# First attention in two parts, three query tiles between the rounds of the last key choice, and the bias table made early

## The reference

```python
def dsa_mixer(h, rel_bias, w_in, ..., w_uq, w_q_idx, w_uk, w_uv, w_o):
    c_q, c_kv, k_idx, w_idx = split(h @ w_in)            # then each normed
    q = einsum('btr,rhd->bthd', c_q, w_uq)
    q_abs = einsum('bthd,chd->bthc', q, w_uk) * HEAD_DIM ** -0.5
    q_idx = einsum('btr,rhd->bthd', c_q, w_q_idx)
    def block(args):                                     # 128 queries
        rel = relu(einsum('bqhd,bsd->bqhs', qi, k_idx))
        score = einsum('bqh,bqhs->bqs', wi, rel)         # causal mask
        _, sel = top_k(score, 128)
        logits = einsum('bqhc,bqkc->bqhk', qa, c_kv[sel]) + rel_bias[rel_bucket(dist)]
        p = masked_softmax(logits, dist >= 0)
        return einsum('bqhk,bqkc->bqhc', p, c_kv[sel])
    o_lat = 4 blocks of 128 queries
    return einsum('bthc,chd->bthd', o_lat, w_uv) @ w_o
```

## Time and profile before

| | us |
|---|---|
| median of 3 runs | 2306.21 (2305.78 to 2306.37) |
| the profiled execution, its own time | 2308.32 |
| its span, first to last instruction | 2306.2 |
| TensorE busy, share of the span | 2260.0 (98%) |
| VectorE busy | 1121.2 (49%) |
| ScalarE busy | 867.4 (38%) |
| POOL busy | 378.9 (16%) |

### The profile page before, as it was taken

How to read it: one execution, slowest core, us unless ns; L and a number is a source line. 1 busy time by engine, 2 the same in 40 slices (tenths; PEclk the granted TensorE clock), 3 DMA queues, 4 the chain that set the end, 5 groups by cost and what they waited for, 6 DMA issues and landing times.

```text
span 2306.2 us, 26051 instructions
## 1 busy us (share of the span) xinstructions
PE 2260.0 (98%) x10833; PEld 1834.2 (80%) x10833; DVE 1121.2 (49%) x1727; ACT 867.4 (38%) x1287; POOL 378.9 (16%) x332
## 2 busy tenths in 40 slices
PE   7999999999999999999999989999999999999998
PEld 6568888888876678888888868888888888888887
DVE  4974433434335645344345566554333446565553
ACT  5673222223225633122134375442322344243343
POOL 0431110112200012011032303332101211000020
PEclk9799999999999999999999999999999999999999
DMA  4203322322261022322346523234255233332331
GB/s 139 101 1 117 103 92 93 108 92 92 96 192 36 1 75 91 108 93 92 95 92 92 37 37 65 47 47 82 55 101 98 94 92 92 110 92 92 100 107 58
DMA packets 221954, 196.26 MB, mean 85 GB/s; under 512 B 7264, under 2 KB 215596, under 8 KB 221709
## 3 DMA queue, kind: packets, MB, share of 16 engines
q1 hardware_dynamic: 220301, 189.08, 31.2%
q0 software_dynamic: 1504, 5.51, 0.7%
q10 hardware_dynamic: 32, 0.01, 0.0%
HBM read 189.87 MB, written 4.72 MB: 84 GB/s over the span
## 4 chain that ended last, share of the span: by engine, by line
PE 89%; DVE 6%; ACT 3%; DMA 1%; issue 1%; POOL 0%; SPq 0%; DVEq 0%; POOLq 0%; ACTq 0%
PE bank L541 24%; PE bank L543 24%; PE bank L542 24%; PE bank L2259 5%; PE bank L2445 2%; PE bank L864 2%; DVE dsa_latents L1217 1%; PE bank L1718 1%; DVE small L1215 1%; PE bank L715 1%; PE bank L725 1%; PE bank L848 1%; ACT hybrid_step L828 1%; PE bank L1335 1%; DVE weight_lo L527 1%
## 5 line engine op out<-in xcount | busy, mean ns | idle before, releaser
L541 PE MATMUL bank<-h_hi,weight_hi 128*128 128x512 f32 (+1 forms) x1568 | 616.0, 393 | 4.7 <-DVE h_lo L647 3.6
L543 PE MATMUL bank<-h_hi,weight_lo 128*128 128x512 f32 (+1 forms) x1568 | 612.1, 390 | 0.0
L542 PE MATMUL bank<-h_lo,weight_hi 128*128 128x512 f32 (+1 forms) x1568 | 611.8, 390 | 0.0
L527 DVE TENSOR_TENSOR weight_lo<-weight_raw,weight_hi 128x2048 fp32r<-128x2048 f32 (+4 forms) x180 | 380.5, 2115 | 362.5 <-ACT weight_hi L518 362.5
L518 ACT ACTIVATE weight_hi<-weight_raw 128x2048 fp32r<-128x2048 f32 (+4 forms) x181 | 317.9, 1757 | 336.3 <-PE bank L543 312.9
L541 PEld LDWEIGHTS bank<-h_hi,weight_hi 128*128 128x128 f32 (+1 forms) x1568 | 294.5, 188 | 69.0 <-issue 7.6
L543 PEld LDWEIGHTS bank<-h_hi,weight_lo 128*128 128x128 f32 (+1 forms) x1568 | 294.4, 188 | 63.3
L542 PEld LDWEIGHTS bank<-h_lo,weight_hi 128*128 128x128 f32 (+1 forms) x1568 | 294.6, 188 | 61.8 <-issue 0.2
L541 PE MATMUL bank<-hidden_hi,weight_hi 128*128 128x512 f32 x512 | 201.8, 394 | 0.0
L543 PE MATMUL bank<-hidden_hi,weight_lo 128*128 128x512 f32 x512 | 200.7, 392 | 0.0
L542 PE MATMUL bank<-hidden_lo,weight_hi 128*128 128x512 f32 x512 | 198.7, 388 | 0.0
(11 more groups left out here) (419 smaller groups left out, 3117.9 us busy)
## 6 DMA issues: line engine op xcount, KB each, us to landing
weight_raw<-in_w_down SPq DMA_DIRECT2D x40, 1024.0 KB, 5.2
weight_raw<-in_w_up SPq DMA_DIRECT2D x32, 1024.0 KB, 5.4
weight_raw<-in_w_up SPq DMA_DIRECT2D x44, 512.0 KB, 5.0
weight_raw<-in_w_in SPq DMA_DIRECT2D x20, 1024.0 KB, 9.2
weight_raw<-in_w_in SPq DMA_DIRECT2D x24, 512.0 KB, 7.0
weight_raw<-in_w_kv_shared SPq DMA_DIRECT2D x6, 1024.0 KB, 4.9
weight_raw<-in_w_branch SPq DMA_DIRECT2D x6, 1024.0 KB, 5.1
weight_raw<-in_a_w_o SPq DMA_DIRECT2D x4, 1024.0 KB, 5.7
```

The lines of the kernel that those rows point to most:

```text
L527: dve.e.tensor_tensor(split_flat(v, 1), raw_flat(v), f32(split_flat(v, 0)), ALU.subtract).then_inc(*split.mark(("unit", v)))
L541: pe.e.matmul(o, w[0], x[0], start=start, stop=False)
L542: pe.e.matmul(o, w[0], x[1], start=False, stop=False)
L543: return pe.e.matmul(o, w[1], x[0], start=False, stop=stop)
```

## The change

The bias table is made before the index queries: two matmuls give the 8 x 640 numbers on 8 partitions, POOL writes them to `bias_line` in DRAM, and one DMA from DRAM to DRAM repeats each line 128 times into `skew`. The sheared load into `bias` follows in POOL's queue after the second tile's score, and the `uq` subtraction goes there too, before the third tile's additions; ScalarE rounds `uq` and takes the root of `ckv` before the third tile's ReLUs. The fold of `ckv` moves into choice 1 and `normed_latents` into choice 2.

The attention is cut in two parts, `early` (query tiles 0 to 2, 384 queries) and `late` (tile 3). The jobs are the eight heads of `early`, then the eight of `late`, in one pipeline of 16 jobs. VectorE's first seven steps stand inside choice 3, one after each two rounds. The rounding of the first `a_o` unit moves from before the attention to pipeline step 11, its split from step 8 (after head 7's maxima) to step 12. `late` has one addend per head; the two-step addition of head 0, tile 3 is gone.

```diff
+        bias_line = nc.dram_tensor("bias_line", [HEADS, N_SHIFT], F32, kind="Internal")
...
         def dsa_tensor(pe):
...
             sums("kidx", 64)
+            pe.wait_ge(*hot_in.when("hot"))
+            pe.wait_ge(*rel_in.when("rel"))
+            pe.wait_ge(*dsa.dve.when("neg"))
+            for n, (c0, c1) in enumerate(BIAS_PARTS):
+                bank = open_bank(pe, ("bias", n), (dsa.act, ("bias", n)))
+                pe.e.matmul(bank[0:HEADS, 0:c1 - c0], rel, one_hot[:, c0:c1], start=True, stop=True
+                            ).then_inc(*dsa.pe.mark(("bias", n)))
...
-            for h in range(HEADS):
-                for half in range(2):
-                    bank = open_bank(pe, ("bias", h, half), (dsa.act, ("bias", h, half)))
-                    pe.e.matmul(bank[:, 0:w], rel_wide[0:BUCKETS + 1, h, :], one_hot[:, half * w:half * w + w], start=True,
-                                stop=True).then_inc(*dsa.pe.mark(("bias", h, half)))
...
         def dsa_scalar(act):
...
+            for n, (c0, c1) in enumerate(BIAS_PARTS):
+                act.wait_ge(*dsa.pe.when("bias", n))
+                act.e.activation(bias_row[0:HEADS, c0:c1], banks.of("bias", n)[0:HEADS, 0:c1 - c0], ACT.Copy
+                                 ).then_inc(*dsa.act.mark(("bias", n)))
             scalar_fold(act, dsa, "kidx", latent_factors["kidx"], 1.0 / IDX_DIM)
...
-            act.e.activation(rel_wide[0:BUCKETS + 1], rel.unsqueeze(2).broadcast_to([BUCKETS + 1, HEADS, P]), ACT.Copy
-                             ).then_inc(*dsa.act.mark(("rel_wide",)))
...
+                elif i == 3:
+                    round_upto(act, unit_at["uq", 0])
+                    scalar_fold(act, dsa, "ckv", latent_factors["ckv"], 1.0 / KV_LORA)
...
-            round_upto(act, unit_at["uq", 0])
-            scalar_fold(act, dsa, "ckv", latent_factors["ckv"], 1.0 / KV_LORA)
-            w = N_SHIFT // 2
-            for h in range(HEADS):
-                for half in range(2):
-                    act.wait_ge(*dsa.pe.when("bias", h, half))
-                    if h > 3:
-                        act.wait_ge(*skew_out[h % 4].when("skew", h - 4))
-                    act.e.activation(bias_rows[h % 4][:, half * w:half * w + w], banks.of("bias", h, half)[:, 0:w], ACT.Copy
-                                     ).then_inc(*dsa.act.mark(("bias", h, half)))
...
-            choose_keys(dve, 1)
-            folded("ckv")
-            dve.wait_ge(*dsa.pool.when("score", 2))
-            choose_keys(dve, 2, lambda: vector_unfold(dve, dsa, "ckv", latent_factors["ckv"], roots))
+            choose_keys(dve, 1, lambda n: folded("ckv") if n == TOP_K // 16 else None)
+            vector_unfold(dve, dsa, "ckv", latent_factors["ckv"], roots)
...
-            dve.wait_ge(*dsa.pool.when("score", 3))
-            choose_keys(dve, 3, normed_latents)
+            dve.wait_ge(*dsa.pool.when("score", 2))
+            choose_keys(dve, 2, lambda n: normed_latents() if n == TOP_K // 16 else None)

         def dsa_pool(pool):
+            for n in range(2):
+                pool.wait_ge(*dsa.act.when("bias", n))
+            pool.e.dma_start(bias_line[:, :], bias_row[0:HEADS]).then_inc(*skew_out.mark(("line",), by=16))
+            pool.wait_ge(*skew_out.when("line"))
+            pool.e.dma_start(skew[:, :, :], bass.AP(tensor=bias_line, offset=0, ap=[[N_SHIFT, HEADS], [0, P], [1, N_SHIFT]])
+                             ).then_inc(*skew_out.mark(("skew",), by=16))
             for i in (2, 3):
...
+                if i == 2:
+                    sheared = bass.AP(tensor=skew, offset=P - 1, ap=[[N_SHIFT - 1, P], [P * N_SHIFT, HEADS], [1, T]])
+                    pool.wait_ge(*skew_out.when("skew"))
+                    pool.e.dma_start(bias[:, :, :], sheared).then_inc(*bias_in.mark(("bias",), by=16))
+                    uq = unit_at["uq", 0]
+                    pool.wait_ge(*rounded.when("unit", uq))
+                    pool.e.tensor_tensor(split_flat(uq, 1), raw_flat(uq), f32(split_flat(uq, 0)), ALU.subtract
+                                         ).then_inc(*dsa.pool.mark(("unit", uq)))
...
+            def vector_scale(self, dve, h):
+                _, den, fac, n = self.stats(h)
+                dve.wait_ge(*self.st.act.when("exp", h, self.tiles[-1]))
+                dve.e.reciprocal(fac[:, n], den[:, n]).then_inc(*self.st.dve.mark())
...
+        early = TileAttention(att0, range(0, NT - 1), 0, 9 * T // 2)
+        late = TileAttention(att0, range(NT - 1, NT), 15 * T, 10 * T)
+        att_jobs = [(early, h) for h in range(HEADS)] + [(late, h) for h in range(HEADS)]
...
         def att0_tensor(pe):
             pe.wait_ge(*dsa.act.when("q_abs", HEADS - 1))
+            pe.wait_ge(*dsa.act.when("ckv_tok"))
+            for n in range(len(att_jobs) + 3):
+                part, h = att_job(n - 2)
+                if part:
+                    part.tensor_turn(pe, h)
+                part, h = att_job(n)
+                if part:
+                    part.tensor_logits(pe, h)
+                part, h = att_job(n - 3)
+                if part:
+                    part.tensor_up(pe, h)
+                part, h = att_job(n - 2)
+                if part:
+                    part.tensor_values(pe, h)
...
         def att0_scalar(act):
+            for n in range(len(att_jobs) + 3):
+                part, h = att_job(n - 2)
+                if part:
+                    part.scalar_turn(act, h)
+                part, h = att_job(n - 3)
+                if part:
+                    part.scalar_attended(act, h)
+                part, h = att_job(n)
+                if part:
+                    part.scalar_exp(act, h)
+                part, h = att_job(n - 2)
+                if part:
+                    part.scalar_latent(act, h)
+                if n == HEADS + 3:
+                    round_upto(act, unit_at["a_o", 0])
...
         def att0_vector(dve):
+            def step(n):
+                part, h = att_job(n - 1)
+                if part:
+                    part.vector_scale(dve, h)
+                part, h = att_job(n - 4)
+                if part:
+                    part.vector_attended(dve, h)
+                part, h = att_job(n)
+                if part:
+                    part.vector_max(dve, h)
+            dve.wait_ge(*dsa.pool.when("score", 3))
             dve.wait_ge(*bias_in.when("bias"))
...
+            choose_keys(dve, 3, lambda n: step(n // 2 - 1) if n % 2 == 0 and n else None)
+            for n in range(HEADS - 1, len(att_jobs) + 4):
+                step(n)
+                if n == HEADS + 4:
                     split_upto(dve, unit_at["a_o", 0])
```

More of the change, by code:

```diff
@@ L999, in build_program @@
         best = small[:, 740:748]
-        bias_rows = [dsa_step(at, N_SHIFT) for at in (6 * T, 6 * T + N_SHIFT, 0, N_SHIFT)]
-        rel_wide = dsa_step(4 * T, HEADS, P)
+        bias_row = dsa_step(4 * T, N_SHIFT)
         A_IN_TILES = [[(0, P), (P, 2 * P)], [(0, P), (P, 200)]]
@@ L1197, in dsa_scalar @@
                     keep_q_abs(h - 2)
-                else:
-                    act.wait_ge(*skew_out[h].when("skew", HEADS - 4 + h))
                 act.wait_ge(*tile_full.when("uq", h))
@@ L1206, in dsa_scalar, with choose_keys @@
                              ).then_inc(*dsa.act.mark(("ckv_tok",)))
-        def choose_keys(dve, i, halfway=None):
+        def choose_keys(dve, i, between):
             S = (i + 1) * P
@@ L1211, in choose_keys @@
             for n in range(TOP_K // 8):
-                if halfway and n == TOP_K // 16:
-                    halfway()
+                between(n)
                 dve.wait_ge(*dsa.dve.last())
@@ L1296, in dsa_pool @@
                                      ).then_inc(*dsa.pool.mark(("score", i)))
-            uq = unit_at["uq", 0]
-            pool.wait_ge(*rounded.when("unit", uq))
-            pool.e.tensor_tensor(split_flat(uq, 1), raw_flat(uq), f32(split_flat(uq, 0)), ALU.subtract
-                                 ).then_inc(*dsa.pool.mark(("unit", uq)))
-            for h in range(HEADS):
-                pool.wait_ge(*dsa.act.when("bias", h, 1))
-                pool.e.dma_start(skew[h], bias_rows[h % 4]).then_inc(*skew_out[h % 4].mark(("skew", h), by=16))
@@ L1304, in dsa_pool @@
-            sheared = bass.AP(tensor=skew, offset=P - 1, ap=[[N_SHIFT - 1, P], [P * N_SHIFT, HEADS], [1, T]])
-            for n in range(4):
-                pool.wait_ge(*skew_out[n].when("skew", HEADS - 4 + n))
-            pool.e.dma_start(bias[:, :, :], sheared).then_inc(*bias_in.mark(("bias",), by=16))
-        att_dsa = Attention(att0, dsa_soft, 0)
-        o_lat = [scratch[0], scratch[1]]
-        addends = [None] + [dsa_soft(16 * T + at, n * P) for n, at in ((2, 0), (3, 2 * P), (4, 5 * P))]
@@ new lines, in att0_tensor @@
+        def att0_tensor(pe):
+            pe.wait_ge(*dsa.act.when("q_abs", HEADS - 1))
+            pe.wait_ge(*dsa.act.when("ckv_tok"))
[12 more added lines that the diff above has]
```

(11 more changed lines are left out.)

174 lines of the change are left out of this document (91 added, 83 removed).

## The result

| | before | after |
|---|---|---|
| median, 6 runs each | 2307.60 us (2305.78 to 2310.42) | 2317.49 us (2315.96 to 2317.89) |
| ratio, 95% interval | | 1.0036 [1.0025, 1.0047] |
| span of the profiled execution | 2306.2 us | 2314.6 us |
| TensorE's mean granted clock | 0.988 | 0.990 |

The interval makes it 5.8 to 10.8 us, against a forecast of 2308 us and a range up to 2314. The first `a_o` product, the number that the change had to move, starts at 184.16 instead of 176.63, 7.5 us later.

What follows compares the result with a forecast made beforehand. VectorE bounds the stage until 122 us, TensorE after it. 23.5 us more of choice 3 against a drain of 33 instead of 54.7 put `a_o` +1.7 later: 2310.0 profiled, 2308 us for plain runs, range 2303 to 2314.

Steps and rivals of the forecast that it cites:

- Step 1: Up to attention's first logits: query product at 86.5 instead of 98.24, logits at 108.2; gain 10.6 us.
- the 0.5 and 0.7 that I had added without a row: Query product and absorptions: 0.5 us for the wait on `ckv_tok`, 0.7 for a clock not warmed by table matmuls.
- Step 2: Choice 3 at head 0: VectorE waits about 8.3 us for logits after two rounds; maxima end at 110.2.
- Step 3: Heads interleaved with choice 3: VectorE needs 35.3 us after head 0's maxima, 5.55 a head, ending at 145.5.
- The clock rival: Interleaved part: TensorE's clock drops to half, +2.1 us a head; four heads +6.7, 2315 us; chance 0.12.
- The estimate of 13 us: Interleaved part: by the skill's clock-oscillation account, 2.1 us lost on all seven heads, some 13 us in all.
- Step 4: Drain from the end of choice 3 at 145.5 to `a_o` at 178.3, +1.7 us against 176.63.
- the tail: End of the drain: exponential, scaling, turn, copy, values, copy and `up` before `a_o`; 4.4 us.
- the `a_o` pair: Drain: `a_o` rounding 1.9 us on ScalarE and splitting 2.3 on VectorE, of which 1.7 remain uncovered.
- the drain loops longer: Drain: exponentials wait behind ScalarE's `up` copies, 0.6 us more for each of eight heads, +4.8; 2313 us; chance 0.13.
- The sum: `a_o` at 178.3, +1.7 us; profiled execution 2310.0 us, less 2.1 for the plain runs' median: 2308 us.
- I had taken 12: Table's DRAM write: 12 us, landed at 61; rival of transfers in series delaying POOL 12 us, 2320 us; chance 0.05.

Runs made afterwards that it cites:

- the run with the gaps shortened: Changed kernel, but during choice 3 VectorE takes each head's `attended` subtraction between two rounds, one round before its step; 2315.05 us, ratio 1.0021 to before.
- The run with the remainder first: Changed kernel, but in every step VectorE does the `attended` subtraction before waiting for exponentials and scaling; 2311.80 us, ratio 1.0008 to before.
- the maxima first: Changed kernel, but from step 7 on VectorE takes head n's maxima before scaling head n-1's rows; 2325.04 us, ratio 1.0067 to before.
- POOL held back: Kernel with maxima before scaling from step 7, plus POOL starting a late head's addend only after VectorE's preceding scaling; 2319.46 us, ratio 1.0044 to before.

## Why the prediction was wrong, step by step

- **Step 1** held. First logits were forecast at 108.2 and came at 109.85, which is 108.7 without the late start. The table costs 1.0 ahead of choice 1 where I took 0.7. From the query product to these logits it took 21.8 us (109.85 - 88.07), 1.25 more than before (118.77 - 98.24), for the 0.5 and 0.7 that I had added without a row; the granted clock is 0.50 in the first 4.9 us of it, 3.4 before. POOL had issued the table's write at 49.8, ahead of the index additions, and nothing on this path waited for it.
- **Step 2** held: 7.5 us for 8.3 at head 0. Choice 3 started at 98.6 without the late start, where I had 97.3; the wait took that up. What I didn't do is ask what those 7.5 us could be spent on; a third of them holds the `a_o` split, and the rest is bought by four more rounds.
- **Step 3** held within 0.6: from the end of head 0's maxima (112.02) to that of choice 3 it took 35.9 us, forecast 35.3. 1.1 of it are the waits at head 5, at half clock. The clock rival happened as a fact of the profile and not as a price in this step: I had given four slow heads 6.7 us, and the run with the gaps shortened got back 1.1 of waits (0.9 of stage), since VectorE's 4.9 to 5.4 us a head cover most of TensorE's slow ones. The Trainium skill ("TensorE: Matmul & The Clock Gate", HAM oscillation) is right here that a loop with such waits drops the clock again and again, three times in 35 us. The estimate of 13 us that I worked out by it for seven heads is refuted: two of the falls lie in this step, and they cost it some 1.1.
- **Step 4 is the one that failed.** I had 32.8 us from the end of choice 3 to `a_o`; it took 36.3. Of the 3.5, scalings beside POOL's addend were 1.0 (1.90 against 0.88), the wait for head 7's exponentials 0.4, waits for the logits of three late heads 1.7 (0.78, 0.55, 0.33), the tail 1.3 (5.7 for 4.4), and the `a_o` pair 0.7 (its split took 3.10 us where the earlier trace rows has 2.29, behind an addend of POOL's that began at 168.75); the rest of the heads were 1.6 better than forecast. The rival "the drain loops longer" named the right engine and order, a copy of an `up` ahead of each exponential, and had 4.8 us for it. I gave it 0.13, because no row of before showed that order. What I hadn't seen is why the copy is late: the bank of `up` rotates onto itself and closes the ring over VectorE. The run with the remainder first takes 3.4 us back, 3.2 of them before the first maximum of the last tile. Not all of it is the ring: that is 0.66 us a head at full clock, and in that run the clock also stays at 1.00 behind the choice. How the rest divides stays open.
- **The sum.** 178.3 became 183.0 at equal start: 0.6, 0.6 and 3.5. The comparison to the median adds what I hadn't carried: the start and the 0.9 us after `a_o`.
- The prediction also didn't ask whether interleaving pays at all. It compared 23.5 us of longer choice with the drain and found them level. The runs say what became of it: two parts cost 5.9 us of stage against one, and what interleaving took from one kind of wait it gave to another. Of the 5.9, the `a_o` pair (2.2, measured with interleaving) and VectorE's order (3.0, measured without) make 5.2 if they add up.

## What to carry to other kernels

Sum the pacing engine's waits over the stage, by what they wait for, before and after. Interleaving shifts waits, and gains only what their total falls by, as long as the engine's own work stays the same; check that too, for with the maxima first it grew from 62 to 67 us (94.1 - 26.9) by the stretched scalings. Start the interleaved work when its first operand is there, not as early as the loop allows, and put independent work where a wait must stay. Where banks rotate, count how many a step opens: if it is all of them, each waits for its own reader of one step ago, and that reader should come first in its engine's step.

## What the runs showed of the hardware

- VectorE's scaling (one operand from SBUF) stands still while POOL's two-operand addition runs: 1.53 us against 0.49 for 512 columns, 1.90 against 0.88 for three tiles, and 1.66 against 0.47 for the comparison beside the `uq` subtraction. Beside the same additions MAX8 of 512 columns keeps its 0.69 and the row maximum of 384 its 0.55. It was the side that started second that waited. This agrees with the Trainium skill, "SBUF — State Buffer", section "SBUF: two separate sides", which has one exclusive lock shared by the two engines. That a wait which looks idle can keep two such instructions apart, worth 1.0 us a head here, was new to me.
- It works the other way too: with POOL held back, one addend of 1.27 us took 3.38 beside VectorE's 2.3 us split of a weight.
- TensorE's granted clock fell to 0.50 during or within 1.5 us of idle gaps of 2.8, 3.5 and 2.7 us and was back at 1.00 some 4 to 6 us after their ends. After gaps of 0.9, 1.2 and 1.7 us it didn't fall.
- One DMA that writes the table of 2.6 MB from DRAM to DRAM landed in 16.3 us, with 207 to 215 GB/s on the core's DMA engines from 54 to 64 us. I had taken 12; it landed 6 us before POOL issued the load that needs it (49.79 + 16.3 against 72.44).
